# Neighbourhood attention: one pipeline over all 80 units, two query rows scored together

## The chip, the cores and the metric

The kernel runs on one core of one Trainium2 chip. The core has five engines with queues of their own: TensorE (PE in the profile, its weight loads PEld), VectorE (DVE), ScalarE (ACT), GpSimd (POOL) and SyncE (SP), which issues the transfers here. They meet through semaphores only. The metric is the device time of one execution in microseconds.

## The reference, cut to what matters

An encoder layer over two batches (1024 and 256 tokens). Its attention branch works on a grid of 64 columns, so 16 and 4 query rows, with 8 heads of 64 channels:

```python
    qg = q.reshape(shp) * (NA_HEAD_DIM ** -0.5)
    row_start = jnp.clip(r - kh // 2, 0, rows - kh)
    key_rows = row_start[:, None] + jnp.arange(kh)[None, :]
    s = jnp.einsum('brqhd,brkwhd->bhrqkw', qg, k_blk).astype(jnp.float32)
    bias = rpb[:, row_idx[:, None, :, None], col_idx[None, :, None, :]]
    s = s + bias[None].astype(jnp.float32)
    s = jnp.where(col_ok[:, None, :], s, -jnp.inf)
    p = jax.nn.softmax(s.reshape(b, NA_HEADS, rows, GRID_W, kh * GRID_W), axis=-1)
    o = jnp.einsum('bhrqkw,brkwhd->brqhd', p, v_blk)
```

A query row of 64 tokens sees 8 rows of keys (512) in the first batch and 4 rows (256) in the second. Ahead of it stand a norm and the projections, behind it the gates, a recurrent mixer, an output projection and a feed-forward part. All is in float32.

## The kernel before

The program runs in stages, each a block with its own semaphores and a barrier at its end: `front` (norm, queries, keys and values), `attention`, `gates_and_shifted`, `scan_mixer`, `merge_and_feed_forward`. The change is in `attention` alone. There is no scheduler: the order on every engine is the order in which the code is written, and waits on counting semaphores tie the engines together.

`attention` loops over 4 pairs of heads and, in each, over 20 query rows (`ROWS`: 16 wide ones with 512 keys, then 4 narrow ones with 256). A pair and a row make a unit, 80 in all. The two heads of a pair lie on partitions 0 to 63 and 64 to 127. For one unit:

- GpSimd copies the 64 queries in reversed order into `qb` (L1477), two buffers.
- TensorE computes the scores of both heads (L1495), a matmul of 64 rows and 64 columns each, head 0 in the first quarter of the array, head 1 in the one diagonally across. Both write the same bank, `at_s`, two buffers. In the trace each float32 matmul is two passes.
- VectorE adds the bias, scales by -1/8 and takes the row's minimum (L1553, named CUSTOM_DVE_ANT_0 in the trace), reading the scores from PSUM and writing `pr`, four buffers.
- ScalarE takes the exponential and its row sum (L1532).
- VectorE inverts the sum (L1561) and multiplies `pr` by it (L1566, the normalising).
- TensorE transposes `pr` in blocks of 128 (L1504) into `at_t`; ScalarE copies that to `prT` (L1539).
- TensorE multiplies with the values (L1517), two halves of the columns at a time, into `at_o`; VectorE writes the result back in the queries' order (L1572).

TensorE's order in step r of a pair is scores of r, transposes of r-2, values of r-3. Each pair of heads begins with an empty pipeline and ends by emptying it (`NR + 3` steps); ScalarE runs the pairs as a loop in hardware (`Fori`). In the second pair GpSimd also splits 2 x 4 parts of gate weights, loaded by SyncE at the start of the stage (L1457), into a high and a low part (L1467, L1470): these are for the next stage.

The bias in SBUF has head 0 of a pair on the first 64 partitions and head 1 on the others.

Of the kernel before, what the change touches and what calls it, by code (L numbers as in the profile page):

```python
# [5 lines left out]
F32, F32R = mybir.dt.float32, mybir.dt.float32r  # L6
ACT = mybir.ActivationFunctionType
ALU = mybir.AluOpType
# [1413 lines left out]
def attention(nc, params, w_in, bias, v_even, v_odd, ident, qk, oT, at_r, gate_w, gate_raw):  # L1422
# [15 lines left out]
    with ExitStack() as ctx:  # L1438
        zero = params[:, PM_ZERO:PM_ZERO + 1]
        put = lambda n, floats, shape: placed(nc, "at_" + n, at_r + 4 * (NODD * CT * P + floats), shape)  # L1440
        sem = lambda n: ctx.enter_context(nc.semaphore("at_" + n))
        pr = [put(f"pr{j}", j * 512, [P, 512]) for j in range(NB)]
# [3 lines left out]
        pb = lambda n: [ctx.enter_context(nc.psum_tensor(f"at_{n}{j}", [P, 512], F32)) for j in range(2)]  # L1446
        s_ps, t_ps, o_ps = pb("s"), pb("t"), pb("o")
        w_ld, high_done, split = [sem(f"w_ld{j}") for j in range(2)], sem("high"), sem("split")
        q_ready, scores, biased, exped, summed, normed = (
            sem("q"), sem("scores"), sem("biased"), sem("exp"), sem("sum"), sem("norm"))  # L1450
        turned, turned_c, pv_done, o_ready = sem("turned"), sem("turned_c"), sem("pv"), sem("o")
        block = ctx.enter_context(nc.Block())

        @block.sync
        def _(sp):
            for j in range(2):
                sp.dma_start(gate_raw[j], w_in[E_G0 + j * KD, :, :]).then_inc(w_ld[j], 16)  # L1457

        @block.gpsimd
        def _(pool):  # L1460
# [12 lines left out]
            for p in range(CT):  # L1473
                for r, (q0, k0, nk, dr) in enumerate(ROWS):
                    n, j = p * NR + r, r % 2
                    pool.wait_ge(scores, n + 1)
                    nc.gpsimd.tensor_copy(qb[j][:, ::-1], qk[:, p, q0:q0 + GRID_W]).then_inc(q_ready, 1)  # L1477
                    if p == 1 and r % 2 and r < 4 * PARTS:
                        split_part(r // 2)
            pool.wait_ge(split, 2 * PARTS)  # L1480

        @block.tensor
        def _(pe):
            pe.sem_inc(scores, 2)
            pe.sem_inc(turned, NB)
            pe.sem_inc(pv_done, 2)
            for p in range(CT):
                for step in range(NR + 3):
                    if step < NR:
                        q0, k0, nk, dr = ROWS[step]  # L1490
                        n, j = p * NR + step, step % 2
                        pe.wait_ge(q_ready, n + 1)
                        pe.wait_ge(biased, n + 1)
                        for rows in heads:
                            last = nc.tensor.matmul(s_ps[j][rows, 0:nk], qb[j][rows, :],  # L1495
                                                    qk[rows, p + CT, k0:k0 + nk], start=True, stop=True)
                        last.then_inc(scores, 1)
                    if 2 <= step <= NR + 1:
                        r = step - 2
                        nk, n, j, b = ROWS[r][2], p * NR + r, r % 2, r % NB  # L1500
                        pe.wait_ge(normed, n + 1)
                        pe.wait_ge(turned_c, n + 1)
                        for m in range(nk // P):
                            last = nc.tensor.transpose(t_ps[j][:, m * P:(m + 1) * P],  # L1504
                                                       pr[b][:, m * P:(m + 1) * P], ident)
                        last.then_inc(turned, 1)
                    if step >= 3:
                        r = step - 3
                        (q0, k0, nk, dr), n, j = ROWS[r], p * NR + r, r % 2
                        pe.wait_ge(turned_c, n + 3)  # L1510
                        pe.wait_ge(o_ready, n + 1)
                        for m in range(nk // P):
                            at = k0 + m * P
                            v = v_even[:, at // P, :] if at % P == 0 else v_odd[:, (at - GRID_W) // P, :]
                            v = v[:, p * P:(p + 1) * P]
                            for rows in heads:
                                last = nc.tensor.matmul(  # L1517
                                    o_ps[j][rows, 0:GRID_W], v[:, rows],
                                    prT[j][:, m * P + rows.start:m * P + rows.stop],
                                    start=m == 0, stop=m == nk // P - 1)  # L1520
                        last.then_inc(pv_done, 1)

        @block.scalar
        def _(act):
            act.sem_inc(exped, NB)
            act.sem_inc(turned_c, 2)
            with act.Fori(0, CT) as p:
                for step in range(NR + 2):
                    if step < NR:
                        nk, n, b = ROWS[step][2], p * NR + step, step % NB  # L1530
                        act.wait_ge(biased, n + 3)
                        nc.scalar.activation(pr[b][:, 0:nk], pr[b][:, 0:nk], ACT.Exp, scale=-1.0, bias=st[b][:, 1:2],  # L1532
                                             accum_out=st[b][:, 2:3]).then_inc(exped, 1)
                    if step >= 2:
                        r = step - 2
                        nk, n, j = ROWS[r][2], p * NR + r, r % 2
                        act.wait_ge(turned, n + (1 + NB))
                        act.wait_ge(pv_done, n + 1)
                        nc.scalar.activation(prT[j][:, 0:nk], t_ps[j][:, 0:nk], ACT.Copy  # L1539
                                             ).then_inc(turned_c, 1)  # L1540

        @block.vector
        def _(dve):
            dve.sem_inc(biased, 2)
            dve.sem_inc(o_ready, 2)
            for p in range(CT):
                for step in range(NR + 3):
                    if step < NR:
                        q0, k0, nk, dr = ROWS[step]
                        n, j, b = p * NR + step, step % 2, step % NB  # L1550
                        dve.wait_ge(scores, n + 3)
                        dve.wait_ge(turned, n + 1)
                        nc.vector.tensor_tensor_reduce(  # L1553
                            pr[b][:, 0:nk], s_ps[j][:, 0:nk],
                            bias[:, bass.ds(p, 1), dr * GRID_W:dr * GRID_W + nk].squeeze(1), -HD ** -0.5, 3.0e38,
                            ALU.add, ALU.min, st[b][:, 1:2]).then_inc(biased, 1)
                    if 1 <= step <= NR:
                        r = step - 1
                        nk, n, b = ROWS[r][2], p * NR + r, r % NB
                        dve.wait_ge(exped, n + (1 + NB))  # L1560
                        nc.vector.reciprocal(st[b][:, 3:4], st[b][:, 2:3]).then_inc(summed, 1)  # L1561
                    if 1 <= step <= NR:
                        r = step - 1
                        nk, n, b = ROWS[r][2], p * NR + r, r % NB
                        dve.wait_ge(summed, n + 1)
# [740 lines left out]
```

## Time and profile before

| | |
|---|---|
| median of 3 runs | 2590.03 us (2589.66 to 2591.17) |
| profiled execution, its own time | 2591.35 us |
| its span, first to last instruction | 2589.6 us |
| TensorE busy in the span | 2465.6 us (95%) |
| VectorE, ScalarE, GpSimd busy | 45%, 28%, 31% |
| attention, first score weights to the next stage's | 199.30 to 367.17 us |

The profile is one execution. The shares of busy time are means over five stages with different limits, so they say little on a change to one of them: the rows that matter are those of the stretch from 199 to 367 us. A busy TensorE is not one at its peak, since the ends of pipelined matmuls are modelled; the distance from the start of one kind of matmul to the start of the next is the better measure of what a group takes.

### The profile page before, as it was taken

How to read it: one execution, taken by the hardware profiler on the slowest of the kernel's cores; microseconds unless marked ns; L12 is line 12 of the kernel's file. 1: busy time of each engine (PE TensorE's matmuls, PEld its weight loads, DVE VectorE, ACT ScalarE, POOL GpSimd, SP SyncE). 2: the span in 40 equal slices, each digit the busy share in tenths (PEclk: the TensorE clock that was granted, in tenths of full speed). 3: DMA queues.
4: the chain of work that ended last, by engine and by line, in shares of the span. 5: the costliest groups of instructions: out<-in, count | busy, mean ns of one | idle time of the engine just before them, and what ended most of it. 6: DMA issues, size and time to landing. Idle time of an engine off the chain costs nothing. (4 is left out here: it accounts for less than half of the span.)

```text
span 2589.6 us, 63095 instructions
## 1 busy us (share of the span) xinstructions
PE 2465.6 (95%) x27732; PEld 2043.4 (79%) x27732; DVE 1176.8 (45%) x2490; ACT 720.8 (28%) x1804; POOL 806.5 (31%) x623
## 2 busy tenths in 40 slices
PE   7999999999999699999999889999999999999997
PEld 6785568888888588888888767878888888888885
DVE  3106650000333566665766575554444444444446
ACT  5115651111111455545545432211110001110013
POOL 3322122222231233333333273023333223332234
PEclk9999999999999799999999989999999999999999
DMA  6110011111110100000000062211111010111114
GB/s 166 45 33 18 1 50 73 66 73 71 36 41 25 43 4 4 4 4 4 4 4 4 3 252 90 90 49 49 41 37 38 33 49 33 41 42 33 33 66 146
DMA packets 39085, 123.08 MB, mean 48 GB/s; under 512 B 11424, under 2 KB 11424, under 8 KB 37664
## 3 DMA queue, kind: packets, MB, share of 16 engines
q1 hardware_dynamic: 38816, 119.06, 13.5%
q8 instruction: 221, 3.62, 0.6%
q14 instruction: 48, 0.39, 0.0%
HBM read 96.24 MB, written 20.97 MB: 45 GB/s over the span
## 5 line engine op out<-in xcount | busy, mean ns | idle before, releaser
L2143 DVE TENSOR_TENSOR ff_f<-ff_f,ff_ps 128x512 f32<-128x512 f32 x300 | 205.3, 686 | 173.8 <-PE ff_ps L98 173.8
L2060 ACT ACTIVATE ff_rl<-ff_ps 128x512 f32<-128x512 f32 (+1 forms) x96 | 50.5, 526 | 756.4 <-PE ff_ps L98 756.4
L2162 DVE TENSOR_TENSOR ff_sq<-ff_rl 128x512 f32<-128x512 f32 (+1 forms) x96 | 124.2, 1294 | 274.7 <-ACT ff_rl L2060 274.6
L1058 DVE TENSOR_TENSOR sc_q<-sc_ps,sc_cs 128x128 f32<-128x128 f32 x400 | 98.7, 281 | 195.9 <-PE sc_ps L465 193.9
L1929 POOL TENSOR_TENSOR ff_wd0h<-ff_wdr,params 128x1024 fp32r<-128x1024 f32 x16 | 30.3, 1894 | 459.4 <-DMA ff_wdr<-in_w_down 459.4
L815 ACT ACTIVATE sc_xy<-sc_ps 128x256 f32<-128x256 f32 x320 | 116.5, 387 | 176.4 <-PE sc_ps L481 173.4
L481 PE MATMUL sc_ps<-sc_xy,sc_q 64*64 64x64 f32 x3200 | 151.5, 222 | 5.1 <-DVE sc_q L1058 4.3
L98 PE MATMUL ff_ps<-hh,ff_wu0h 128*128 128x512 f32 (+1 forms) x384 | 137.0, 357 | 4.5 <-issue 4.5
L98 PE MATMUL ff_ps<-hh,ff_wu0l 128*128 128x512 f32 (+1 forms) x384 | 136.9, 356 | 0.0
L98 PE MATMUL ff_ps<-hl,ff_wu0h 128*128 128x512 f32 (+1 forms) x384 | 136.9, 356 | 0.0
L98 PE MATMUL ff_ps<-hh,ff_wu1h 128*128 128x512 f32 (+1 forms) x384 | 136.3, 355 | 0.0
L98 PE MATMUL ff_ps<-hl,ff_wu1h 128*128 128x512 f32 (+1 forms) x384 | 136.2, 355 | 0.0
L98 PE MATMUL ff_ps<-hh,ff_wu1l 128*128 128x512 f32 (+1 forms) x384 | 135.8, 354 | 0.0
L481 PEld LDWEIGHTS sc_ps<-sc_xy,sc_q 64*64 64x64 f32 x3200 | 128.3, 138 | 7.5 <-DVE sc_q L1058 5.2
L1553 DVE CUSTOM_DVE_ANT_0 at_pr<-at_s,sT 128x512 f32<-128x512 f32 (+1 forms) x80 | 51.0, 638 | 170.7 <-PE at_s L1495 170.7
L98 PE MATMUL ff_ps<-ff_wd0h,ff_gh 128*128 128x512 f32 x320 | 124.8, 390 | 1.8 <-DVE ff_f L2143 1.8
L465 PEld LDWEIGHTS sc_ps<-sc_xy,sc_ai 64*64 64x64 f32 x3200 | 76.3, 134 | 63.1 <-issue 28.3
L477 PE MATMUL sc_ps<-sc_q,sc_xy 64*64 64x64 f32 x2560 | 120.5, 234 | 5.8 <-DVE sc_q L1058 3.7
L1747 DVE TENSOR_TENSOR gp_gm<-gp_sg,gp_ps 128x512 f32<-128x512 f32 (+1 forms) x24 | 14.4, 598 | 245.2 <-PE gp_ps L98 245.2
L98 PE MATMUL ff_ps<-ff_wd0l,ff_gh 128*128 128x512 f32 x320 | 124.6, 389 | 0.0
L98 PE MATMUL ff_ps<-ff_wd1h,ff_gh 128*128 128x512 f32 x320 | 124.6, 389 | 0.0
L98 PE MATMUL ff_ps<-ff_wd1l,ff_gh 128*128 128x512 f32 x320 | 124.5, 389 | 0.0
(323 smaller groups left out, 7004.7 us busy)
## 6 DMA issues: line engine op xcount, KB each, us to landing
ff_wur<-in_w_up SPq DMA_DIRECT2D x32, 512.0 KB, 3.4
ff_wdr<-in_w_down SPq DMA_DIRECT2D x32, 512.0 KB, 4.3
gwr<-in_w_in SPq DMA_DIRECT2D x31, 512.0 KB, 3.5
gm_dram<-gp_gm SPq DMA_DIRECT2D x8, 1280.0 KB, 4.4
ff_m<-gm_dram SPq DMA_DIRECT2D x16, 640.0 KB, 7.6
fr_x<-in_x SPq DMA_DIRECT2D x10, 512.0 KB, 4.9
ff_xs<-in_x SPq DMA_DIRECT2D x10, 512.0 KB, 4.4
x_dram<-ff_xo SPq DMA_DIRECT2D x10, 512.0 KB, 2.9
```

The source lines that it names most:

```text
L98: mm = nc.tensor.matmul(out, stationary[a], moving[b], start=first and n == 0, stop=last and n == len(pairs) - 1)
L465: last = nc.tensor.matmul(q_out[g][across(rows, u), u, :], AI[g][rows, u, :], XY[g][rows, X_AT, u, :], start=True, stop=True)
L477: nc.tensor.matmul(x_out[g][rows, u, :], XY[g][at, Y_AT, u, :], Q1[g][at, u, :], start=True, stop=True)
L481: last = nc.tensor.matmul(y_out[g][rows, u, :], Q1[g][rows, u, :], XY[g][rows, Y_AT, u, :], start=True, stop=True)
L815: nc.scalar.activation(XY[g][:, :, :, :].rearrange("p n u t -> p n (u t)"), yx_out[g], ACT.Copy).then_inc(xy_ready, 1)
L1058: nc.vector.tensor_tensor(Q1[g][:, :, :], q_out[g], joins[:, l, :].rearrange("p (u t) -> p u t", u=2), ALU.mult).then_inc(q_ready, 1)
L1553: nc.vector.tensor_tensor_reduce(pr[b][:, 0:nk], s_ps[j][:, 0:nk], bias[:, bass.ds(p, 1), dr * GRID_W:dr * GRID_W + nk].squeeze(1), -HD ** ...
L1747: nc.vector.tensor_tensor(gm[c % 2][:, 0, t0:t0 + tn], sga[:, t0:t0 + tn], ps[:, u % 8, 0:tn], ALU.mult).then_inc(merged, 1)
L1929: nc.gpsimd.tensor_tensor(high, w_raw[m], zero_like(high, zero), ALU.add).then_inc(high_done, 1)
L2060: nc.scalar.activation(rl[v % 2][:, 0:tn], ps[:, b, 0:tn], ACT.Relu).then_inc(relu, 1)
L2143: nc.vector.tensor_tensor(own, own, ps[:, 4 + v % 4, :], ALU.add).then_inc(added, 1)
L2162: nc.vector.tensor_tensor(sq[v % 2][:, 0:tn], rl[v % 2][:, 0:tn], rl[v % 2][:, 0:tn], ALU.mult).then_inc(squared, 1)
```

## The change

- **One pipeline.** The 80 units run through without emptying between pairs of heads; `unit(n)` gives pair and row of unit n. ScalarE's hardware loop is written out.
- **Two rows at once.** TensorE scores the units 2k and 2k+1 together: four matmuls on the four quarters of the array. Unit 2k keeps its heads where they were, in unit 2k+1 the heads are exchanged (`half_of`): head 0's scores lie on partitions 64 to 127. There are four score buffers in place of two, and both units read their keys and queries from the same partitions.
- **Bias copy.** Odd units need the bias with heads exchanged. SyncE copies it inside SBUF, pair by pair, into `bias_x` (two buffers, two transfers of 64 partitions x 896 numbers per pair). The loads of the gate weights stand behind the copies of the first two pairs, and VectorE waits for the copy before the bias step of an odd unit.
- **Normalising on GpSimd.** The multiplication by the inverse sum goes from VectorE to GpSimd, whose order in a step is: normalise 2k-2, copy queries 2k+2 and 2k+3, normalise 2k-1, and in every third step one part of the gate weights.
- **Order.** TensorE's step k: scores of 2k and 2k+1, transposes of 2k-3, values of 2k-4, transposes of 2k-2, values of 2k-3. VectorE: bias of n, output of n-5, inverse of n-1. ScalarE: copy of n-3, exponential of n.

The core of the diff:

```diff
+        bias_x = [put(f"bx{j}", (NB + 2) * 512 + 2 * GRID_W + 8 * NB + j * TURN, [P, TURN]) for j in range(2)]
+        pb = lambda n, k: [ctx.enter_context(nc.psum_tensor(f"at_{n}{j}", [P, 512], F32)) for j in range(k)]
+        s_ps, t_ps, o_ps = pb("s", 4), pb("t", 2), pb("o", 2)
...
+        UNITS, STEPS_A = CT * NR, CT * NR // 2
+
+        def unit(n):
+
+            return (n // NR,) + ROWS[n % NR]
+
+        def half_of(n, h):
+
+            return heads[h if n % 2 == 0 else 1 - h]
 
         @block.sync
         def _(sp):
-            for j in range(2):
-                sp.dma_start(gate_raw[j], w_in[E_G0 + j * KD, :, :]).then_inc(w_ld[j], 16)
+            for p in range(CT):
+                if p >= 2:
+                    sp.wait_ge(biased, (p - 1) * NR)
+                for h in range(2):
+                    sp.dma_start(bias_x[p % 2][heads[1 - h], :], bias[heads[h], p, 0:TURN]).then_inc(bx_in[p % 2], 16)
+                if p == 1:
+                    for j in range(2):
+                        sp.dma_start(gate_raw[j], w_in[E_G0 + j * KD, :, :]).then_inc(w_ld[j], 16)
...
-            for p in range(CT):
-                for r, (q0, k0, nk, dr) in enumerate(ROWS):
-                    n, j = p * NR + r, r % 2
-                    pool.wait_ge(scores, n + 1)
-                    nc.gpsimd.tensor_copy(qb[j][:, ::-1], qk[:, p, q0:q0 + GRID_W]).then_inc(q_ready, 1)
-                    if p == 1 and r % 2 and r < 4 * PARTS:
-                        split_part(r // 2)
+            def queries(n):
+                p, q0 = unit(n)[0:2]
+                if n >= 2:
+                    pool.wait_ge(scores, n // 2)
+                nc.gpsimd.tensor_copy(qb[n % 2][:, ::-1], qk[:, p, q0:q0 + GRID_W]).then_inc(q_ready, 1)
+
+            def normal(n):
+                nk, b = unit(n)[3], n % NB
+                pool.wait_ge(summed, n + 1)
+                nc.gpsimd.tensor_scalar(pr[b][:, 0:nk], pr[b][:, 0:nk], st[b][:, 3:4], None, ALU.mult
+                                        ).then_inc(normed, 1)
+
+            queries(0)
+            queries(1)
+            for k in range(STEPS_A + 1):
+                if k >= 1:
+                    normal(2 * k - 2)
+                if k + 1 < STEPS_A:
+                    queries(2 * k + 2)
+                    queries(2 * k + 3)
+                if k >= 1:
+                    normal(2 * k - 1)
+                if k % 3 == 0 and 0 < k // 3 <= 2 * PARTS:
+                    split_part(k // 3 - 1)
...
+            def score(k):
+                pe.wait_ge(q_ready, 2 * k + 2)
+                if k >= 2:
+                    pe.wait_ge(biased, 2 * k - 2)
+                for h in range(2):
+                    for n in (2 * k, 2 * k + 1):
+                        p, q0, k0, nk, dr = unit(n)
+                        last = nc.tensor.matmul(s_ps[n % 4][half_of(n, h), 0:nk], qb[n % 2][heads[h], :],
+                                                qk[heads[h], p + CT, k0:k0 + nk], start=True, stop=True)
+                last.then_inc(scores, 1)
+
+            def turn(n):
+                nk = unit(n)[3]
+                pe.wait_ge(normed, n + 1)
+                if n >= 2:
+                    pe.wait_ge(turned_c, n - 1)
+                for m in range(nk // P):
+                    last = nc.tensor.transpose(t_ps[n % 2][:, m * P:(m + 1) * P],
+                                               pr[n % NB][:, m * P:(m + 1) * P], ident)
+                last.then_inc(turned, 1)
+
+            def values(n):
+                p, q0, k0, nk, dr = unit(n)
+                pe.wait_ge(turned_c, n + 1)
+                if n >= 2:
+                    pe.wait_ge(o_ready, n - 1)
+                for m in range(nk // P):
+                    at = k0 + m * P
+                    v = v_even[:, at // P, :] if at % P == 0 else v_odd[:, (at - GRID_W) // P, :]
+                    v = v[:, p * P:(p + 1) * P]
+                    for h in range(2):
+                        mine = half_of(n, h)
+                        last = nc.tensor.matmul(
+                            o_ps[n % 2][heads[h], 0:GRID_W], v[:, heads[h]],
+                            prT[n % 2][:, m * P + mine.start:m * P + mine.stop],
+                            start=m == 0, stop=m == nk // P - 1)
+                last.then_inc(pv_done, 1)
+
+            for k in range(STEPS_A + 2):
+                if k < STEPS_A:
+                    score(k)
+                for a in (2 * k - 3, 2 * k - 2):
+                    if 0 <= a < UNITS:
+                        turn(a)
+                    if 0 <= a - 1 < UNITS:
+                        values(a - 1)
...
+            for n in range(UNITS + 3):
+                if n >= 3:
+                    copied(n - 3)
+                if n < UNITS:
...
-                        dve.wait_ge(summed, n + 1)
-                        nc.vector.tensor_scalar(pr[b][:, 0:nk], pr[b][:, 0:nk], st[b][:, 3:4], None,
-                                                ALU.mult).then_inc(normed, 1)
...
+            def biases(n):
+                p, q0, k0, nk, dr = unit(n)
+                b, at = n % NB, slice(dr * GRID_W, dr * GRID_W + nk)
+                dve.wait_ge(scores, n // 2 + 1)
+                if n >= NB:
+                    dve.wait_ge(turned, n - NB + 1)
+                if n % 2:
+                    dve.wait_ge(bx_in[p % 2], 32 * (p // 2 + 1))
+                nc.vector.tensor_tensor_reduce(
+                    pr[b][:, 0:nk], s_ps[n % 4][:, 0:nk], bias_x[p % 2][:, at] if n % 2 else bias[:, p, at],
+                    -HD ** -0.5, 3.0e38, ALU.add, ALU.min, st[b][:, 1:2]).then_inc(biased, 1)
...
+            for n in range(UNITS + 5):
+                if n < UNITS:
+                    biases(n)
+                if n >= 5:
+                    out_rows(n - 5)
+                if 1 <= n <= UNITS:
+                    inverse(n - 1)
+            dve.wait_ge(o_ready, UNITS)
```

On TensorE, in the middle of the first pair of heads, before (`at_s` scores, `at_t` transposes, `at_o` values; the number behind a buffer's name tells which one it is):

```order
L1495 MATMUL at_s<-sT,at_qb_1433 64x512 x2
L1504 MATMUL at_t<-cn,at_pr_1429 128x128 x4
L1517 MATMUL at_o<-at_prT_1432,v_odd 64x64 x8
L1495 MATMUL at_s<-sT,at_qb_1434 64x512 x2
L1504 MATMUL at_t<-cn,at_pr_1430 128x128 x4
L1517 MATMUL at_o<-at_prT_1431,v_even 64x64 x8
```

and now:

```order
L1526 MATMUL at_s<-sT,at_qb_1433 64x512
L1526 MATMUL at_s<-sT,at_qb_1434 64x512
L1526 MATMUL at_s<-sT,at_qb_1433 64x512
L1526 MATMUL at_s<-sT,at_qb_1434 64x512
L1536 MATMUL at_t<-cn,at_pr_1428 128x128 x4
L1551 MATMUL at_o<-at_prT_1431,v_even 64x64 x8
L1536 MATMUL at_t<-cn,at_pr_1429 128x128 x4
L1551 MATMUL at_o<-at_prT_1432,v_odd 64x64 x8
```

The scores of two units stand together, those of both query buffers in turn; transposes and values follow twice.

On GpSimd, where gate weights are split, before (`at_qb` the query copies, `gw0h` and `gw0l` the two parts of a gate weight):

```order
L1477 COPY at_qb_1433<-sT 128x64
L1477 COPY at_qb_1434<-sT 128x64
L1467 TENSOR_TENSOR gw0h<-gwr_71,params 128x256
L1470 TENSOR_TENSOR gw0l<-gwr_71,gw0h 128x256
L1477 COPY at_qb_1433<-sT 128x64
```

and now:

```order
L1495 COPY at_qb_1434<-sT 128x64
L1500 TENSOR_SCALAR at_pr_1428<-at_pr_1428,at_st_1436 128x512
L1500 TENSOR_SCALAR at_pr_1429<-at_pr_1429,at_st_1437 128x512
L1495 COPY at_qb_1433<-sT 128x64
L1495 COPY at_qb_1434<-sT 128x64
L1500 TENSOR_SCALAR at_pr_1430<-at_pr_1430,at_st_1438 128x512
L1485 TENSOR_TENSOR gw0h<-gwr_71,params 128x256
L1488 TENSOR_TENSOR gw0l<-gwr_71,gw0h 128x256
L1500 TENSOR_SCALAR at_pr_1427<-at_pr_1427,at_st_1435 128x512
L1495 COPY at_qb_1433<-sT 128x64
```

A split now stands between two normalisings, and query copies stand behind a normalising.

On SyncE, at the start of the stage, as a difference (`at_bx` the bias with heads exchanged, `gwr` the gate weights):

```order
-L1454 UNCONDITIONAL_BRANCH
-L1457 DMA gwr_71<-in_w_in 128x1024
-L1457 DMA gwr_72<-in_w_in 128x1024
+L1466 UNCONDITIONAL_BRANCH
+L1472 DMA at_bx_1439<-sT 64x896 x2
+L1472 DMA at_bx_1440<-sT 64x896 x2
+L1475 DMA gwr_71<-in_w_in 128x1024
+L1475 DMA gwr_72<-in_w_in 128x1024
+L1472 DMA at_bx_1439<-sT 64x896 x2
+L1472 DMA at_bx_1440<-sT 64x896 x2
```

The gate loads moved behind four copies; the last four wait for bias steps of earlier pairs.

## Rows read from the trace of the kernel before

**Rows 1.** Busy time (instructions): PE, PEld, DVE, ACT, POOL; then clock, DMA, GB/s.

```profile
199.00:367.00 168.00, 163.35 (x1760) 86.07 (x1760) 108.30 (x400) 102.89 (x244) 31.14 (x96) 1.00 0.02 8
```

**Rows 2.** Timeline at the stage's two ends: start, duration, engine, what [idle before, releaser].

```profile
198.66 0.80 SPq L1457 DMA_DIRECT2D gwr<-in_w_in  x2
199.30 0.22 PEld L1495 LDWEIGHTS at_s<-sT,at_qb 64*64 64x64 f32 x4 [1.69 <-POOL at_qb L1477]
...
366.43 0.23 DVE L1572 TENSOR_SCALAR sT<-at_o 128x64 f32<-128x64 f32 x1 [0.32 <-PE at_o L1517]
367.17 0.19 PEld L98 LDWEIGHTS gp_ps<-hh,gw0h 128*128 128x128 f32 x1 [0.92 <-issue]
```

**Rows 3.** Timeline of one wide unit's time in the first pair.

```profile
229.83 1.08 PE L1495 MATMUL at_s<-sT,at_qb 64*64 64x512 f32 x4
...
230.84 0.65 PE L1504 MATMUL at_t<-cn,at_pr 128*128 128x128 f32 x4
230.96 0.69 DVE L1553 CUSTOM_DVE_ANT_0 at_pr<-at_s,sT 128x512 f32<-128x512 f32 x1 [0.78 <-PE at_s L1495]
...
231.43 0.69 PE L1517 MATMUL at_o<-at_prT,v_even 128*64 128x64 f32 x16
...
231.57 0.16 DVE L1561 RECIPROCAL at_st<-at_st 128x1 f32<-128x1 f32 x1
231.69 0.72 ACT L1532 ACTIVATE at_pr<-at_pr,at_st 128x512 f32<-128x512 f32 x1 [0.91 <-DVE at_st L1553]
...
232.04 0.65 PE L1495 MATMUL at_s<-sT,at_qb 64*64 64x256 f32 x4
232.17 0.22 DVE L1572 TENSOR_SCALAR sT<-at_o 128x64 f32<-128x64 f32 x1
...
232.41 0.57 ACT L1539 ACTIVATE at_prT<-at_t 128x512 f32<-128x512 f32 x1
```

**Rows 4.** Timeline, TensorE, narrow units of the first and the last pair.

```profile
237.16 0.65 PE L1495 MATMUL at_s<-sT,at_qb 64*64 64x256 f32 x4
...
237.74 0.44 PE L1504 MATMUL at_t<-cn,at_pr 128*128 128x128 f32 x2
...
238.11 0.45 PE L1517 MATMUL at_o<-at_prT,v_even 128*64 128x64 f32 x8
...
364.64 0.45 PE L1517 MATMUL at_o<-at_prT,v_even 128*64 128x64 f32 x8
365.02 0.20 PEld L1504 LDWEIGHTS at_t<-cn,at_pr 128*128 128x128 f32 x2
```

**Rows 5.** Timeline, TensorE, in the scan: four quarters at once.

```profile
1001.33 0.46 PE L465 MATMUL sc_ps<-sc_xy,sc_ai 64*64 64x64 f32 x16
1001.61 0.28 PE L532 MATMUL sc_ps<-sc_gm,sc_vt 64*64 64x64 f32 x4
```

**Rows 6.** GpSimd: one tile's operation (ns min/median/max), two groups (busy us, mean ns).

```profile
L299 POOL TENSOR_SCALAR sc_fac<-sc_icl,params,sc_k1a x19: 767/768/770, 881.6 to 1419.7; 128x512 f32<-128x512 f32 x19
...
L1920 POOL TENSOR_TENSOR hl<-ff_m,hh 128x512 fp32r<-128x512 f32 x16 | 24.8, 1569 | 15.3 <-ACT hh L2023 15.3
...
L1477 POOL COPY at_qb<-sT 128x64 f32<-128x64 f32 x80 | 19.5, 245 | 150.0 <-PE at_s L1495 129.4 <-PEq L1484 20.6
```

**Rows 7.** A split on GpSimd (timeline), and two VectorE operations (ns min/median/max).

```profile
243.90 0.72 POOL L1470 TENSOR_TENSOR gw0l<-gwr,gw0h 128x256 fp32r<-128x256 f32 x1
...
L1553 DVE CUSTOM_DVE_ANT_0 at_pr<-at_s,sT x80: 423/691/693, 200.4 to 363.3; 128x512 f32<-128x512 f32 x64, 128x256 f32<-128x256 f32 x16
...
L1566 DVE TENSOR_SCALAR at_pr<-at_pr,at_st x80: 352/487/1002, 202.2 to 364.5; 128x512 f32<-128x512 f32 x64, 128x256 f32<-128x256 f32 x16
```

**Rows 8.** Transfers: what, queue, count, KB each, median us from issue to landing.

```profile
v_odd<-v_even SPq DMA_DIRECT2D x2, 896.0 KB, 8.3
```

**Rows 9.** Front stage: a wait of TensorE in the timeline, and the stretch behind it.

```profile
80.27 0.50 PE L98 MATMUL fr_ps<-fr_wvh,hh 128*128 128x512 f32 x1 [3.85 <-POOL hl L1370]
...
80.00:86.00 6.00, 5.74 (x18) 4.58 (x19) 0.00 (x0) 0.00 (x0) 0.21 (x1) 0.72 0.00 0
```

More of the change, by code:

```diff
@@ L1445, in attention @@
         st = [put(f"st{j}", (NB + 2) * 512 + 2 * GRID_W + 8 * j, [P, 4]) for j in range(NB)]
[L1446 to L1447 removed]
+        bias_x = [put(f"bx{j}", (NB + 2) * 512 + 2 * GRID_W + 8 * NB + j * TURN, [P, TURN]) for j in range(2)]
+        pb = lambda n, k: [ctx.enter_context(nc.psum_tensor(f"at_{n}{j}", [P, 512], F32)) for j in range(k)]
+        s_ps, t_ps, o_ps = pb("s", 4), pb("t", 2), pb("o", 2)
         w_ld, high_done, split = [sem(f"w_ld{j}") for j in range(2)], sem("high"), sem("split")
+        bx_in = [sem(f"bx{j}") for j in range(2)]
         q_ready, scores, biased, exped, summed, normed = (
@@ L1483, in _ @@
         def _(pe):
[L1484 to L1521, printed above, removed]
@@ L1523, in _ @@
+            for k in range(STEPS_A + 2):
[6 more added lines that the diff above has]
+                        values(a - 1)
         @block.scalar
         def _(act):
[L1525 to L1540, printed above, removed]
@@ new lines, in copied @@
+            def copied(n):
+                nk, j = unit(n)[3], n % 2
+                act.wait_ge(turned, n + 1)
+                if n >= 2:
+                    act.wait_ge(pv_done, n - 1)
+                nc.scalar.activation(prT[j][:, 0:nk], t_ps[j][:, 0:nk], ACT.Copy).then_inc(turned_c, 1)
+            for n in range(UNITS + 3):
+                if n >= 3:
+                    copied(n - 3)
+                if n < UNITS:
+                    nk, b = unit(n)[3], n % NB
+                    act.wait_ge(biased, n + 1)
+                    nc.scalar.activation(pr[b][:, 0:nk], pr[b][:, 0:nk], ACT.Exp, scale=-1.0, bias=st[b][:, 1:2],
+                                         accum_out=st[b][:, 2:3]).then_inc(exped, 1)
@@ L1542, in _ @@
         @block.vector
         def _(dve):
[L1544 to L1564, printed above, removed]
-                        dve.wait_ge(summed, n + 1)
-                        nc.vector.tensor_scalar(pr[b][:, 0:nk], pr[b][:, 0:nk], st[b][:, 3:4], None,
-                                                ALU.mult).then_inc(normed, 1)
-                    if step >= 3:
-                        r = step - 3
-                        q0, n, j = ROWS[r][0], p * NR + r, r % 2
-                        dve.wait_ge(pv_done, n + 3)
-                        nc.vector.tensor_scalar(oT[:, bass.ds(p, 1), q0:q0 + GRID_W],
-                                                o_ps[j][:, GRID_W - 1::-1], 1.0, None,
-                                                ALU.mult).then_inc(o_ready, 1)
@@ new lines, in inverse, with out_rows @@
+            def inverse(n):
+                b = n % NB
+                dve.wait_ge(exped, n + 1)
+                nc.vector.reciprocal(st[b][:, 3:4], st[b][:, 2:3]).then_inc(summed, 1)
+            def out_rows(n):
+                p, q0 = unit(n)[0:2]
+                dve.wait_ge(pv_done, n + 1)
+                nc.vector.tensor_scalar(oT[:, p, q0:q0 + GRID_W], o_ps[n % 2][:, GRID_W - 1::-1], 1.0, None,
+                                        ALU.mult).then_inc(o_ready, 1)
+            for n in range(UNITS + 5):
[5 more added lines that the diff above has]
+                    inverse(n - 1)
```

2 lines of the change are left out of this document (1 added, 1 removed).

## The prediction

> **What bounds the kernel now.** The change lies in one stage only, so I read that stage alone. The busy time by stretch [rows 1] comes first: of the 168 us in which the attention runs, TensorE is busy for 163.35, VectorE for 108.30, ScalarE for 102.89 and GpSimd for 31.14. TensorE is the bound, the others have room. The rows at the edges of the stage [rows 2] give its length: the first weight load of the scores starts at 199.30, the first one of the next stage at 367.17, so 167.87 us. Then one unit (two heads, one query row) in order of time [rows 3]: TensorE's block of score passes starts at 229.83, the four transposes at 230.84, the passes over the values at 231.43, and the next scores at 232.04. These starts give slots that hold the drain between kinds of matmul too: scores 1.01, transposes 0.59, values 0.61, together 2.21 us, with nothing between them. VectorE shows idle time of 0.78 before its bias step at 230.96 and was released by the scores: it waits for TensorE, not the other way round. For a narrow unit (256 keys) the slots are 0.58 for scores (237.16 to 237.74), 0.37 for transposes (237.74 to 238.11) and 0.38 for values (364.64 to 365.02) [rows 4].
>
> A check that these slots are the stage: a head pair has 16 wide and 4 narrow units, so 16 x 2.21 + 4 x 1.33 = 40.7 us of TensorE, four pairs make 162.7. The stage takes 167.87, so 5.2 us are left for filling and emptying the pipeline at five ends of a pair and for the step into the next stage.
>
> **The scores.** One step now scores two units: eight passes over all four quarters instead of two blocks of four passes over two. Per pair of heads that is 8 wide and 2 narrow blocks instead of 16 and 4. What a block of eight costs is not in the trace at 512 columns. The nearest rows are the scan's L465 [rows 5]: sixteen passes of 64 columns on all four quarters, every second pair reading the same rows of the array with another moving operand, take 0.28 us until the next kind starts. That is 16 x 64 / 0.28 = 3.7 columns per ns, against 4 x 512 / 1.01 = 2.0 for the scores now, which use two quarters. So four quarters do run at once, at nearly twice the rate of two. Lower bound for the new block: that of two quarters, 1.01. By the rate of L465 alone it is 8 x 512 / 3.7 = 1.12 (its starting and draining time scaled up with it). The other end is no overlap, 2.02. I take 1.02, since L465's short blocks carry start and drain eight times as heavily; 0.60 for a narrow one. Scores per pair of heads: now 16 x 1.01 + 4 x 0.58 = 18.5; then 8 x 1.02 + 2 x 0.60 = 9.4. Four pairs: 36.5 us less. With 1.12 it would be about 3 us less than that.
>
> The Trainium skill, page "TensorEngine Tiling (Array Packing)", section "Restrictions and Gotchas", speaks against this: it says that different row tiles cannot access the same PSUM bank at the same time. By that rule the two heads of a unit, which sit in the two row halves and write one bank, would run one after the other, the new block would take 2.0 us and the stage would gain nothing from it. L465 also writes one bank from both row halves and the row above shows it at the four-quarter rate, so the trace does not bear the rule out here; what it would give is the first rival.
>
> **Transposes and values** keep their passes: 16 x 1.20 + 4 x 0.75 = 22.2 us per pair of heads, 88.8 in all. TensorE's work is then 126.2 us in place of 162.7, and a step of two wide units is 1.02 + 2 x 1.20 = 3.42.
>
> **Does the rest keep up with 3.42?** I count from the end of a score block, step k, times as in [rows 3], 0.05 to 0.1 for each handover. ScalarE: an exponential, its accumulator read and a copy follow each other in 0.72 + 0.58 = 1.30, so 2.6 per step. VectorE loses the normalising pass (0.49) and keeps bias 0.69, inverse 0.16 and output 0.22: 2.2 per step. GpSimd gets the normalising: its TENSOR_SCALAR on 128x512 takes 0.77 on this engine (L299), and the slowest operation of that shape, with two inputs, 1.57 (L1920) [rows 6]. The former is the same operation with one more arithmetic step, so 0.77; with two query copies of 0.245 it is 2.0 per step, or 3.6 with 1.57. In 8 of the 40 steps a split of gate weights is queued behind a normalising, two operations of the kind of L1470 at 0.72 [rows 7]: 3.5 in such a step, behind which the next normalising waits.
>
> Latency, for unit 2k: the transposes of 2k-3 end at about 0.65, their copy 0.7 to 1.3, the exponential of 2k to 2.0, its accumulator to 2.2, the inverse to 2.4, the normalising on GpSimd to 3.2. The transposes of 2k stand at 3.42 + 1.20 = 4.6: 1.4 us to spare, about 0.3 in a step with a split (normalising 3.5 to 4.3). For unit 2k+1 the transposes come another 2.2 us later. The query copies of the next step are queued on GpSimd behind a normalising that was released a step before, and are done by 0.6, where the scores want them at 2.4. So no wait enters a wide step. Narrow steps last 0.60 + 2 x 0.75 = 2.1 and have less room, while latencies shrink with the width; if each of the 8 lost 0.5, that is 4 us, which goes into the range.
>
> VectorE's old normalising pass was the one slowed by GpSimd: 1.00 at worst, beside a split, where it takes 0.49 otherwise [rows 7]. It goes; the longest of all 80 bias steps is 0.693, so splits do not touch these.
>
> **The start** gets worse. SyncE issued the gate weights at 198.66 [rows 2]; these now stand behind four copies of bias with heads exchanged, and VectorE's second bias step waits for the first two of them. In VectorE's queue the inverse of unit 0 stands behind that step, so GpSimd's normalising and the first transposes wait for it as well. The nearest copy inside SBUF is that of v_odd: two of 896 KB, 8.3 us to landing [rows 8]. Two of 224 KB move a quarter: between 2.1 (all of it scales) and 8.3 (none); I take 4.3, so 203. Then bias, inverse and normalising (0.69 + 0.16 + 0.77 and handovers) let the first transposes start at 205, while TensorE has both first score blocks done at 201.4: 3.6 us idle. With the early landing it is 1.7, with the late one 7.6. An idle stretch of this length lowered the clock once: TensorE stood still for 3.85 us until 80.27, and from 80 to 86 the granted clock was 0.72 on the mean, which is 3.4 us at the lower level of 1.2 GHz and a loss of 6 x 0.28 = 1.7 us [rows 9]. I count half of it, 0.8, as it may fall either way.
>
> **The end**: the transposes of the last units wait some 0.4 for their normalising, then the last output and the step to the next stage as now, 0.9 from the last values (366.43 to 367.17 and the handover) [rows 2]. The three inner joints between pairs of heads are gone, since steps run through. Filling and emptying: 0.2 (the second query copy) + 3.6 + 0.8 + 0.4 + 0.9 = 5.9, against 5.2.
>
> **Sum.** 36.5 - 0.7 = 35.8 us. The gate weights are split within the stage as before, the next stage starts with the same loads, so what is won here stays won: the profiled execution of 2591.35 would be 2555.6, and the median of the runs, 2590.03, stands at 2554.2. I predict 2554. With early landing, no clock loss: 2551 or a little less. With 1.12 per block, late landing, a full clock loss and narrow steps that wait: 2566.
>
> **Rivals.**
> First: quarters that share rows or a bank do not overlap at 512 columns. For it: no row shows four streams that long. Against it: L465. A block takes 2.0, TensorE's work is 162.7 again, only joints change by a microsecond: 2589 to 2592. The change would then not do what it says. Chance 0.08. (The page named above speaks for it too.)
> Second: the loop through four engines has a wait that I have not seen. For it: there is one more handover (VectorE to GpSimd), and strict order on VectorE puts the inverse behind the output of an older unit. Against it: 1.4 us of room in the ordinary step. A wait of 0.3 to 0.5 in each of 40 steps is 12 to 20 us: 2566 to 2574. Chance 0.10.
> Third, slower than before: GpSimd becomes the bound. A step of before costs 2 x 2.21 = 4.42, so it decides from 2 N + 0.49 = 4.42, N = 1.97 us for a normalising. That the two engines stretch each other is seen in [rows 7], by a factor of two at worst (VectorE's 487 ns became 1002); that gives N = 1.54, a step of 3.57 and some 5 us, no more. A factor of three, N = 2.3, gives a step of 5.1, 0.7 above the old one in 32 wide steps: 2612. Against it: the 19 runs of L299 take 767 to 770 ns beside a busy VectorE [rows 6], and VectorE's remaining operations read PSUM. Chance 0.04.
>
> **How the numbers follow.** The forecast has 0.78 (2549 to 2563), the second rival 0.10, the first 0.08, the third 0.04. The range of 2548 to 2569 holds the forecast with its unknown costs and part of the second rival. A measurement of this kernel tells a difference from about 0.2%, 5 us: faster 0.88 (forecast and second rival), same 0.08, slower 0.04.
>
> **What would show it.** Score blocks that start to transposes in 1.02 and steps of 3.42 show the first term right; 2.0 shows the first rival. Idle time of TensorE before transposes, released by GpSimd, in the middle of the stage is the second; GpSimd busy for the whole stage with normalisings over 1.5 us is the third. The first transposes at 205 and VectorE released by a DMA before its second bias step show the start right. The first load of the next stage should stand at 331 to 332. I am wrong if that is later than 345.

## The result, and the profile after

| | before | after |
|---|---|---|
| median | 2590.60 us (4 runs, 2589.66 to 2593.42) | 2573.06 us (4 runs, 2570.69 to 2575.41) |
| ratio to before | | 0.993, 95% interval 0.9913 to 0.9948 |
| attention, first score weights to the next stage's first weights | 167.87 us | 148.00 us |

The kernel is faster by 17.5 us where the prediction had 36, and its time lies outside the predicted range (2548 to 2569). The attention gave back 19.9 us of the 35.8 that were summed up for it. The prediction's own sign of being wrong came, too: the next stage starts at 348.78, later than 345.

```profile
200.78 0.21 PEld L1526 LDWEIGHTS at_s<-sT,at_qb 64*64 64x64 f32 x8 [1.54 <-POOL at_qb L1495]
...
348.78 0.19 PEld L98 LDWEIGHTS gp_ps<-hh,gw0h 128*128 128x128 f32 x1 [0.92 <-issue]
```

The stretch of the attention, busy time by engine as in [rows 1] (PE, PEld, DVE, ACT, POOL, then clock, DMA, GB/s):

```profile
199.00:348.00 149.00, 131.60 (x1764) 79.94 (x1763) 69.67 (x319) 97.84 (x242) 138.22 (x176) 0.98 0.08 21
```

GpSimd went from 31 us to 138 of 149 us. It is the busiest engine now, and TensorE, which was busy for nearly all of the stage in [rows 1], is idle for 17 us of it. Who waits for whom in this stretch (us in total, times, longest):

```profile
PEld at_t L1536 <- POOL at_pr L1500: 45.3, 56, 4.3
...
PE at_t L1536 <- POOL at_pr L1500: 15.0, 18, 3.4
```

The transposes wait for the normalising on GpSimd. The groups by line show why (busy us, mean ns of one | idle before):

```profile
L1500 POOL TENSOR_SCALAR at_pr<-at_pr,at_st 128x512 f32<-128x512 f32 x64 | 99.8, 1568 | 3.9 <-DVE at_st L1601 3.9
L1536 PE MATMUL at_t<-cn,at_pr 128*128 128x128 f32 x288 | 50.2, 293 | 15.4 <-POOL at_pr L1500 15.0
...
L1500 POOL TENSOR_SCALAR at_pr<-at_pr,at_st 128x256 f32<-128x256 f32 x16 | 14.7, 927 | 1.4 <-DVE at_st L1601 1.4
```

One normalising takes 1.57 us, not the 0.77 that the scan's TENSOR_SCALAR of the same shape took in [rows 6]. With it GpSimd has hardly a gap: ahead of its 64 wide normalisings it sat idle for 3.9 us in all, most of it before the first one. Two steps in order of time, PE and GpSimd only:

```profile
290.58 1.09 PE L1526 MATMUL at_s<-sT,at_qb 64*64 64x512 f32 x8
291.60 0.42 PEld L1536 LDWEIGHTS at_t<-cn,at_pr 128*128 128x128 f32 x4 [0.81 <-POOL at_pr L1500]
...
292.70 0.42 POOL L1495 COPY at_qb<-sT 128x64 f32<-128x64 f32 x2
...
293.08 1.58 POOL L1500 TENSOR_SCALAR at_pr<-at_pr,at_st 128x512 f32<-128x512 f32 x1
...
294.02 1.09 PE L1526 MATMUL at_s<-sT,at_qb 64*64 64x512 f32 x8
294.62 0.62 POOL L1485 TENSOR_TENSOR gw1h<-gwr,params 128x256 fp32r<-128x256 f32 x1
...
295.32 0.73 POOL L1488 TENSOR_TENSOR gw1l<-gwr,gw1h 128x256 fp32r<-128x256 f32 x1
...
296.03 1.57 POOL L1500 TENSOR_SCALAR at_pr<-at_pr,at_st 128x512 f32<-128x512 f32 x1
297.54 0.41 POOL L1495 COPY at_qb<-sT 128x64 f32<-128x64 f32 x2
297.64 0.42 PEld L1536 LDWEIGHTS at_t<-cn,at_pr 128*128 128x128 f32 x4 [1.47 <-POOL at_pr L1500]
...
298.85 1.09 PE L1526 MATMUL at_s<-sT,at_qb 64*64 64x512 f32 x8
```

The score block of two units takes 1.02 (290.58 to 291.60), as predicted. The first step lasts 3.44 (290.58 to 294.02): two normalisings and two copies keep GpSimd busy for all of it, and TensorE's work in a step, 3.42, is about as long. In the second, GpSimd splits a part of the gate weights, 1.4 us, and nothing hides that: the normalising behind it ends at 297.6, the transposes start then, and the step lasts 4.83.

The start of the stage in order of time: the copies, the second bias step, the first transposes, the third score block:

```profile
200.30 2.45 SPq L1472 DMA_DIRECT2D at_bx<-sT  x4
...
204.41 0.69 DVE L1594 CUSTOM_DVE_ANT_0 at_pr<-at_s,at_bx 128x512 f32<-128x512 f32 x1 [1.77 <-DMA at_bx<-sT]
...
206.90 0.71 PEld L1536 LDWEIGHTS at_t<-cn,at_pr 128*128 128x128 f32 x4 [4.26 <-POOL at_pr L1500]
...
207.95 1.99 PE L1526 MATMUL at_s<-sT,at_qb 64*64 64x512 f32 x8
```

The copy was there 4.1 us after the queue began to issue (4.3 in the sum). The score block at 207.95 takes 1.99 instead of 1.09: the granted clock was at its lower level, 1.2 GHz, for 6.8 us from 205.7. The fall came while TensorE waited for the first normalising (3.4 us, 203.5 to 206.9).

### The profile page after: what moved, and what is told of

The parts are those of the page before. It is cut to its first block and busy times, and to the rows that moved or that the text cites. A ratio compares the mean times of both kernels' runs of the same rounds, so it can differ in the third digit from the quotient of the medians.

```text
span 2571.2 us, 62946 instructions
## 1 busy us (share of the span) xinstructions
PE 2436.8 (95%) x27732; PEld 2039.2 (79%) x27732; DVE 1142.1 (44%) x2410; ACT 716.5 (28%) x1801; POOL 914.4 (36%) x703
## 5 line engine op out<-in xcount | busy, mean ns | idle before, releaser
L98 PE MATMUL ff_ps<-ff_wd0h,ff_gl 128*128 128x512 f32 x320 | 124.5, 389 | 0.0
L98 PE MATMUL ff_ps<-ff_wd1h,ff_gl 128*128 128x512 f32 x320 | 124.5, 389 | 0.0
```

Source lines behind the costliest of these rows:

```text
L98: mm = nc.tensor.matmul(out, stationary[a], moving[b], start=first and n == 0, stop=last and n == len(pairs) - 1)
```

## Experiments

The theory from here on: GpSimd's time for one normalising sets the step, by its own form. Rivals: it is slow because VectorE works beside it; or it does not matter, and the longer way round through the engines sets the step.

**The form of the operation.** In the changed kernel, behind the last values, GpSimd runs each of nine operations three times, while the other engines have nothing left to do in this stage:

```diff
             pool.wait_ge(split, 2 * PARTS)
+            pool.wait_ge(pv_done, UNITS)
...
+                done(nc.gpsimd.tensor_scalar(pr[0], pr[0], s1, None, ALU.mult))
+                done(nc.gpsimd.tensor_scalar(pr[1], pr[0], s1, None, ALU.mult))
+                done(nc.gpsimd.tensor_scalar(pr[0], pr[0], s1, zero, ALU.mult, ALU.add))
...
+                done(nc.gpsimd.tensor_scalar(pr[1], pr[0], 0.5, None, ALU.mult))
...
+                done(nc.gpsimd.tensor_tensor(pr[3], pr[0], s1.to_broadcast([P, 512]), ALU.mult))
+                done(nc.gpsimd.tensor_copy(pr[1], pr[0]))
```

> Theory A: the normalising on GpSimd is slow by its own form (one arithmetic step, in place: 1.57 us in the changed kernel, where the scan's two-step TENSOR_SCALAR took 0.77). Theory B: it is slow because VectorE works beside it. The changed kernel, with 27 more operations on GpSimd at the end of the attention, when TensorE, VectorE and ScalarE have finished there: 128x512, in place or not, with one or two arithmetic steps, by a column or a constant, a TENSOR_TENSOR and a copy. A expects the in-place one-step form at about 1.57 here too and a two-step one near 0.77; B expects every TENSOR_SCALAR near 0.77. The whole gets some 30 us longer; its time is not compared.

The rows of these lines, ns min/median/max:

```profile
L1527 POOL TENSOR_SCALAR at_pr<-at_pr,at_st x3: 1564/1564/1564, 345.5 to 367.4; 128x512 f32<-128x512 f32 x3
...
L1528 POOL TENSOR_SCALAR at_pr<-at_pr,at_st x3: 1564/1565/1566, 347.1 to 369.1; 128x512 f32<-128x512 f32 x3
...
L1529 POOL TENSOR_SCALAR at_pr<-at_pr,at_st,params x3: 766/767/767, 348.8 to 370.8; 128x512 f32<-128x512 f32 x3
...
L1532 POOL TENSOR_SCALAR at_pr<-at_pr x3: 1490/1490/1490, 351.4 to 373.4; 128x512 f32<-128x512 f32 x3
...
L1533 POOL TENSOR_SCALAR at_pr<-at_pr,params x3: 1573/1575/1575, 353.0 to 374.9; 128x512 f32<-128x512 f32 x3
...
L1534 POOL TENSOR_TENSOR at_pr<-at_pr,at_st x3: 1040/1040/1040, 354.6 to 376.6; 128x512 f32<-128x512 f32 x3
L1535 POOL COPY at_pr<-at_pr x3: 611/611/611, 355.7 to 377.7; 128x512 f32<-128x512 f32 x3
```

The same multiplication takes 1564 ns alone (L1527), in place or into another buffer (L1528), and 767 ns when an addition of zeros is written behind it (L1529). A constant in place of the column changes little (L1532, 1490), and a single addition is as slow (L1533, 1575). So it is the form, and VectorE beside it adds nothing (1568 in the attention).

**That form in the kernel.** The normalising with a second arithmetic step:

```diff
-                nc.gpsimd.tensor_scalar(pr[b][:, 0:nk], pr[b][:, 0:nk], st[b][:, 3:4], None, ALU.mult
-                                        ).then_inc(normed, 1)
+                nc.gpsimd.tensor_scalar(pr[b][:, 0:nk], pr[b][:, 0:nk], st[b][:, 3:4], zero, ALU.mult,
+                                        ALU.add).then_inc(normed, 1)
```

> The changed kernel, with the normalising on GpSimd written with two arithmetic steps (times the inverse, plus a column of zeros), as the scan's operation is. If the one-step form is the slow one (theory A in its narrow sense), a normalising falls from 1.57 to about 0.77 and the time to 2556 to 2560. If in-place writing, or VectorE beside it (B), is the reason, it stays at 1.57 and the time at 2573.

2553.70 us (4 runs, 2553.49 to 2556.32), 0.9851 of before (0.9834 to 0.9867). The normalising, and two score blocks of a step in the middle of the first pair:

```profile
L1500 POOL TENSOR_SCALAR at_pr<-at_pr,at_st,params 128x512 f32<-128x512 f32 x64 | 49.4, 773 | 24.6 <-DVE at_st L1601 24.4
```

```profile
211.49 1.09 PE L1526 MATMUL at_s<-sT,at_qb 64*64 64x512 f32 x8
...
214.91 1.09 PE L1526 MATMUL at_s<-sT,at_qb 64*64 64x512 f32 x8
```

773 ns, steps of 3.42 (211.49 to 214.91), and GpSimd waits again for VectorE. The attention takes 132.2 us. One added arithmetic step is worth 19 us by the medians, 15.8 of them in the attention (148.0 to 132.2). The way round through the engines is the same as in the changed kernel, so its length does not set the step.

**The normalising back on VectorE**, all else as changed:

```diff
-            def normal(n):
-                nk, b = unit(n)[3], n % NB
-                pool.wait_ge(summed, n + 1)
-                nc.gpsimd.tensor_scalar(pr[b][:, 0:nk], pr[b][:, 0:nk], st[b][:, 3:4], None, ALU.mult
-                                        ).then_inc(normed, 1)
...
+            def normal(n):
+                nk, b = unit(n)[3], n % NB
+                dve.wait_ge(summed, n + 1)
+                nc.vector.tensor_scalar(pr[b][:, 0:nk], pr[b][:, 0:nk], st[b][:, 3:4], None, ALU.mult
+                                        ).then_inc(normed, 1)
...
                 if 1 <= n <= UNITS:
                     inverse(n - 1)
+                    normal(n - 1)
```

> The changed kernel with the normalising back on VectorE, all else as changed. If GpSimd's busy time sets the step (A and B alike), TensorE is the bound again: attention about 133 us in place of 148, 2573 - 15 = 2558. Theory C, the longer way round through the engines sets the step whichever engine normalises: the time stays within 4 us of 2573. VectorE as a new bound would be some 3.3 us a step (2 x (0.61 + 0.2 + 0.2 + 0.5) and handovers), still under TensorE's 3.42.

2555.31 us (4 runs, 2553.98 to 2556.60), 0.9856 (0.9839 to 0.9872); the attention takes 131.9 us. Groups by line:

```profile
L1526 PE MATMUL at_t<-cn,at_pr 128*128 128x128 f32 x288 | 49.8, 292 | 1.4 <-DVE at_pr L1596 1.4
...
L1596 DVE TENSOR_SCALAR at_pr<-at_pr,at_st 128x512 f32<-128x512 f32 x64 | 31.3, 489 | 2.3
```

TensorE waits 1.4 us in all ahead of its transposes, against 15.4 in the changed kernel. The way round is shorter here by one handover, so this run alone could not rule it out; the fast form on GpSimd, with the way round of the changed kernel and 2553.70 us, did. The move to GpSimd was not needed for the gain: VectorE has room for it at 0.49 us a unit.

**The splits behind all normalisings.**

```diff
-                if k % 3 == 0 and 0 < k // 3 <= 2 * PARTS:
-                    split_part(k // 3 - 1)
+            for n in range(2 * PARTS):
+                split_part(n)
             pool.wait_ge(split, 2 * PARTS)
```

> The changed kernel with the eight splits of gate weights on GpSimd moved behind all normalisings, to the end of the stage. If GpSimd is busy without a gap in the steps (A, B), the 8 x 1.35 us go from the steps to the end and the time stays within 3 us of 2573. If the steps wait for latency and GpSimd has gaps in which splits hide (C), the end gets 10.8 us longer: 2583 or so.

2571.62 us (4 runs, 2569.05 to 2573.13), 0.9919 (0.9902 to 0.9935), within 1.4 us of the changed kernel; the attention takes 147.4 us against 148.0. What the steps no longer pay, the end pays. From the fourth score block to the last the changed kernel takes 125.14 us (213.41 to 338.55) and this one 115.15 (212.00 to 327.15), so the splits cost 10.0 us there; at the end TensorE now stands still for about as long:

```profile
346.62 0.29 PEld L98 LDWEIGHTS gp_ps<-hh,gw0h 128*128 128x128 f32 x1 [10.19 <-issue]
```

GpSimd's work sets the length of the stage in either order.

**Two quarters.** From the kernel with two arithmetic steps, the heads stay where they are and the two units of a step are scored one after the other on the same two quarters:

```diff
-            return heads[h if n % 2 == 0 else 1 - h]
+            return heads[h]
...
-                for h in range(2):
-                    for n in (2 * k, 2 * k + 1):
-                        p, q0, k0, nk, dr = unit(n)
+                for n in (2 * k, 2 * k + 1):
+                    p, q0, k0, nk, dr = unit(n)
+                    for h in range(2):
...
-                    pr[b][:, 0:nk], s_ps[n % 4][:, 0:nk], bias_x[p % 2][:, at] if n % 2 else bias[:, p, at],
+                    pr[b][:, 0:nk], s_ps[n % 4][:, 0:nk], bias[:, p, at],
```

> As the kernel with two arithmetic steps in the normalising, but the heads are not exchanged in odd units: both units of a step use the same two quarters, first one unit, then the other, and the bias is read from one place (the copies with heads exchanged are still made and waited for). All else, the pipeline over 80 units and the normalising on GpSimd included, stays. If the gain is the quarters' (my sum), a score block of two units takes 2.0 in place of 1.02, TensorE's work is 162.7 again and the time 2589 to 2592. If the through pipeline or the emptied VectorE made the gain, the time stays nearer to 2554 than to 2590.

2583.67 us (7 runs, 2579.06 to 2585.05), 0.9963 (0.9951 to 0.9976), attention 159.3 us. A score block and the transposes behind it:

```profile
215.53 1.93 PE L1526 MATMUL at_s<-sT,at_qb 64*64 64x512 f32 x8
...
217.39 0.42 PEld L1536 LDWEIGHTS at_t<-cn,at_pr 128*128 128x128 f32 x4 [0.81 <-POOL at_pr L1500]
```

The block takes 1.86 where four quarters take 1.02, so the quarters are worth 27 us of the stage (159.3 to 132.2). The pipeline without joints, and blocks of two units, give the other 8.6 us (167.9 to 159.3). That is more than I had put down for it: a step of two wide units takes 4.27 here (211.26 to 215.53), not 2 x 2.21, which is 0.15 in each of 32 steps, 4.8 us. The rest I put down to the joints; no run takes them alone. The expectation of 2589 to 2592 was too high by that.

**The first bias copy a stage earlier.** From the kernel with two arithmetic steps:

```diff
+            sp.wait_ge(bias_ready, 1)
+            for h in range(2):
+                sp.dma_start(first_x[(1 - h) * HD:(2 - h) * HD, :], bias[h * HD:(h + 1) * HD, 0, 0:14 * GRID_W]
+                             ).then_inc(v_moved, 16)
             for e in range(2, E_QK):
                 weights_qk(e)
-            sp.wait_ge(v_moved, 32)
+            sp.wait_ge(v_moved, 64)
...
-            for p in range(CT):
+            for p in range(1, CT):
                 if p >= 2:
                     sp.wait_ge(biased, (p - 1) * NR)
...
-                if n % 2:
-                    dve.wait_ge(bx_in[p % 2], 32 * (p // 2 + 1))
+                if n % 2 and p:
+                    dve.wait_ge(bx_in[p % 2], 32 * ((p + 1) // 2))
```

> As the kernel with two arithmetic steps, but the first pair's bias with heads exchanged is copied in the stage before, behind the bias and ahead of the loads of query and key weights, so that no transfer stands at the start of the attention. There VectorE waited 1.75 us for the copy, and the clock was at its lower level for 6.8 us from 202.4, worth 3.4 us of matmuls. If the wait caused the fall of the clock, both go: 4 to 5 us less, 2549. If the clock falls all the same, only the wait goes: 1.7 us less, 2552.

> The kernel with two arithmetic steps in the normalising again, for the comparison with the early copy on the same chip: 2553 to 2556.

2552.84 us (4 runs, 2552.24 to 2555.64) against 2553.49 (4 runs, 2551.73 to 2555.22) for the kernel without it on the same chip: 0.9847 (0.9831 to 0.9863) and 0.985 (0.9833 to 0.9868) of before. The start of the attention with the early copy:

```profile
201.96 1.99 PE L1530 MATMUL at_s<-sT,at_qb 64*64 64x512 f32 x8 [0.56 <-POOL at_qb L1499]
202.07 0.69 DVE L1598 CUSTOM_DVE_ANT_0 at_pr<-at_s,bx 128x512 f32<-128x512 f32 x1
...
204.14 1.11 PE L1540 MATMUL at_t<-cn,at_pr 128*128 128x128 f32 x4 [0.20 <-POOL at_pr L1504]
```

The wait for the copy is gone: the second bias step starts as soon as the first is done. The clock falls all the same, in the second score block, which takes 1.99 again, so the wait for the copy is not needed for the fall. The attention takes 129.8 us against 132.1 in the one profile of each, and all of that lies at its start (8.4 against 10.7 us to the fourth score block). But behind the attention the profile with the early copy is 2.1 us longer, and the difference of the medians, 0.65 us, is less than the spread of the runs. What this edit brings to the whole kernel is not settled.

**More forms.** As the first, at the end of the attention of the kernel with two arithmetic steps:

```diff
+                done(nc.gpsimd.tensor_scalar(half(pr[1]), half(pr[0]), s1, None, ALU.mult))
+                done(nc.gpsimd.tensor_scalar(half(pr[1]), half(pr[0]), s1, zero, ALU.mult, ALU.add))
+                done(nc.gpsimd.tensor_scalar(pr[1], pr[0], 0.5, 0.0, ALU.mult, ALU.add))
+                done(nc.gpsimd.tensor_scalar(pr[1], pr[0], s1, 1.0, ALU.mult, ALU.mult))
+                done(nc.gpsimd.tensor_scalar(pr[1], pr[0], s1, zero, ALU.mult, ALU.max))
+                done(nc.gpsimd.tensor_scalar(pr[1], pr[0], s1, None, ALU.max))
+                done(nc.gpsimd.tensor_scalar(pr[1], pr[0], s1, None, ALU.subtract))
```

> The kernel with two arithmetic steps in the normalising, with 21 more operations on GpSimd at the end of the attention, when the other engines have finished there: which two-step and one-step TENSOR_SCALARs are fast. If the second step as such makes the difference, all two-step ones of 128x512 (constants, a constant as second operand, times and maximum) take about 0.77 and all one-step ones (maximum, subtract) about 1.57; 128x256 takes 0.93 with one step and 0.56 with two, as in the attention. If the pair times-plus is a special case, the other two-step ones stay near or above 1.57. Its time, some 17 us longer, is not compared.

In the order of the diff's lines from the second on, ns min/median/max:

```profile
L1529 POOL TENSOR_SCALAR at_pr<-at_pr,at_st,params x3: 548/549/554, 333.2 to 350.6; 128x256 f32<-128x256 f32 x3
...
L1530 POOL TENSOR_SCALAR at_pr<-at_pr x3: 617/618/618, 333.9 to 351.2; 128x512 f32<-128x512 f32 x3
...
L1531 POOL TENSOR_SCALAR at_pr<-at_pr,at_st x3: 689/691/691, 334.6 to 351.9; 128x512 f32<-128x512 f32 x3
...
L1532 POOL TENSOR_SCALAR at_pr<-at_pr,at_st,params x3: 2067/2068/2072, 335.4 to 352.7; 128x512 f32<-128x512 f32 x3
...
L1533 POOL TENSOR_SCALAR at_pr<-at_pr,at_st x3: 1562/1567/1567, 337.6 to 354.9; 128x512 f32<-128x512 f32 x3
...
L1534 POOL TENSOR_SCALAR at_pr<-at_pr,at_st x3: 1562/1567/1567, 339.2 to 356.5; 128x512 f32<-128x512 f32 x3
```

Both readings were half right. Times-plus and times-times are fast (0.62 to 0.77), times-maximum is slow (2.07), and the one-step forms are slow again (1.57, maximum and subtract). So a second step does not help as such; certain pairs are fast. What in the engine makes the difference the traces do not show.

## Why the prediction was wrong, point by point

- **The bound and the slots** were right. TensorE set the old stage, and the slots carried over: 1.02 for the block, 3.42 for a step as soon as GpSimd leaves it alone.
- **The scores** were right in size: the block of eight takes 1.02, the value chosen from [rows 5]. The Trainium skill, page "TensorEngine Tiling (Array Packing)", section "Restrictions and Gotchas", says that different row tiles cannot access the same PSUM bank at the same time. The trace does not agree: in every block here two row halves write one bank, and it takes 1.02.
- **The step that failed** is the price of the normalising: "The former is the same operation with one more arithmetic step, so 0.77". It takes 1.57. The row [rows 6] was of another form, and the argument that one step less cannot cost more was never measured: the trace of the kernel before holds no one-step TENSOR_SCALAR on GpSimd. The other end, 1.57 by the slowest row of that shape, stood in the sentence before, and it was the right number by chance, since it is that of an operation with two inputs.
- **The price of that other end was wrong too.** For a normalising of N = 1.54 us the third rival says "a step of 3.57 and some 5 us, no more". Ordinary steps did lose little (3.44 in place of 3.42). But with GpSimd full, the eight splits have nowhere to hide. I had counted them inside a step of 3.5 with N = 0.77 and not again with N = 1.57. A split among wide steps makes one last 4.83 in place of 3.42; some of the eight fell beside narrow steps and cost less. Together they are the 10.0 us above, of a shortfall of 15.8 in the stage (148.0 against 132.2 with the fast form). The rest, by the starts of the score blocks, is 3.1 us of waits, mostly where narrow and wide units meet, 1.9 at the start, where the first normalisings stand on the path, and 0.8 at the end.
- **The start** was right in kind and near in size: the copy landed after 4.1 us (4.3), the first transposes stood back behind it. The clock fell too, in every profile with four quarters, and the prediction had counted half of a fall. It was at the lower level for 6.8 us in the changed kernel and in the first profile of the fast form, and for 3.4 us in the second; the attentions of the last two are 132.2 and 132.1 us, so the longer fall did not show in the stage. A long idle stretch, from which the prediction took this term [rows 9], is not needed for it: in the first profile of the fast form the fall began at 202.4, two microseconds ahead of TensorE's wait for the first normalising, and with the early copy it came with no such wait. A fall at the start of the next stage, 3.4 us from 349.0, was not foreseen; it came in the changed kernel, not with the fast form.
- **The end and the sum.** With the normalising at its predicted 0.77, the whole sum holds: the stage takes 132.2 us (predicted 167.9 - 35.8 = 132.1) and the kernel 2553.5 to 2553.7 (predicted 2554). At the start that is in part luck: the prediction had 3.6 us of idle TensorE before the first transposes and 0.8 of lost clock, and the first profile of the fast form shows 1.7 us of idle there and, on the lower clock, two score blocks of 1.99.
- **The rivals.** The second (a hidden wait) had its symptom, transposes released by GpSimd, but the cause was work and not latency; that the measured 2573 lies in its range of 2566 to 2574 is chance. The third was the right mechanism, at a price between its own: GpSimd as the bound does not make the kernel slower than before at N = 1.57.

## What to carry to other kernels

Before work goes to GpSimd, time the very form there, operation pair and operands included: here one multiplication takes twice as long as a multiplication and an addition. When an engine comes close to full, add up everything queued on it again, the odd jobs as well, since the cheap ones lose their cover first. And a step that is moved to relieve an engine with room to spare buys nothing: the gain was the four quarters and the through pipeline.

## What the runs showed of the hardware

- GpSimd, TENSOR_SCALAR on 128x512 float32, alone: one step 1.49 to 1.58 us (times, plus, minus, maximum), times-plus 0.62 to 0.77, times-times 0.69, times-maximum 2.07; a copy 0.61, a TENSOR_TENSOR with one operand broadcast 1.04. On 128x256 one step takes 0.93, times-plus 0.55.
- Four quarters of the array, with moving operands of 512 columns in float32, two quarters at a time reading the same partitions and two writing the same bank, take 1.02 us for eight passes; on two quarters the same number of passes takes 1.86.
- In every profile with scores on four quarters the clock fell at the start of the attention, for 3.4 to 10.2 us, with and without the wait for the copy; in the two profiles with the scores on two quarters (the kernel before and the run above) it did not. What makes it fall is not shown. The stretch in the changed kernel, with the early copy, and on two quarters (the clock is the third number from the end):

```profile
205.75:212.40 6.65, 5.49 (x34) 3.11 (x35) 2.72 (x13) 3.51 (x10) 6.42 (x8) 0.50 0.38 144
...
202.00:205.30 3.30, 3.10 (x16) 1.09 (x20) 2.23 (x10) 2.08 (x5) 1.55 (x4) 0.50 0.96 284
...
201.00:212.00 11.00, 9.46 (x72) 4.11 (x74) 4.78 (x18) 7.08 (x16) 5.05 (x12) 1.00 0.62 180
```
